# Routed experts on one core: full-width row gathers and scatters without branches, and the down matmul split into high and low parts

## The reference

```python
scores = sigmoid(hf @ w_router); sel = scores + b_router
eidx = top 8 of sel within the best 4 of 8 groups
gw = scores[eidx] / sum * ROUTE_SCALE
for each expert e, with xb = hf[its tokens]:      # xb: n_e x 1024
    u  = silu(xb @ w_gate[e]) * (xb @ w_up[e])    # n_e x 256
    yb = (u @ w_down[e]) * g[:, None]             # n_e x 1024
    y[its tokens] += yb
y += (silu(hf @ ws_gate) * (hf @ ws_up)) @ ws_down
```

## Time and profile before

| | |
|---|---|
| median of 3 runs | 1129.77 us (1128.4 to 1130.07) |
| the profiled execution's own time | 1132.51 us |
| its span in the trace | 1130.7 us |
| mean granted TensorE clock | 0.972 |
| PE busy | 1037.0 us (92%) |
| DVE busy | 836.9 us (74%) |
| ACT busy | 521.8 us (46%) |
| POOL busy | 234.5 us (21%) |
| DMA, all queues | 297.60 MB, 263 GB/s in the mean |
| scatters on the chain that ended last | 28% of the span |

### The profile page before, as it was taken

One profiled execution on the slowest core, in us unless ns is written; L12 is line 12 of the kernel. 1 busy time (PEld: TensorE's weight loads), 2 busy tenths in 40 slices (PEclk: granted clock), 3 DMA queues, 4 the chain that ended last, 5 costly groups with the idle time before them and its releaser, 6 DMA issues.

```text
span 1130.7 us, 16022 instructions
## 1 busy us (share of the span) xinstructions
PE 1037.0 (92%) x4777; PEld 733.0 (65%) x4778; DVE 836.9 (74%) x1480; ACT 521.8 (46%) x610; POOL 234.5 (21%) x145
## 2 busy tenths in 40 slices
PE   1899997978998989999998999999999999899995
PEld 1898887657446447766775666667766666566662
DVE  4887899886665457787876787778787776676865
ACT  3425463364111145555554554555555454545542
POOL 0000000100000034353321323423222222342210
PEclk9899998989996999999999999999999999999998
DMA  9775300600948078999999999999999999999944
GB/s 358 244 277 178 101 1 1 229 14 13 388 186 327 27 249 269 356 344 343 338 366 348 323 333 344 345 337 329 324 338 333 346 308 339 304 328 334 340 113 152
DMA packets 82999, 297.60 MB, mean 263 GB/s; under 512 B 10799, under 2 KB 23131, under 8 KB 73437
## 3 DMA queue, kind: packets, MB, share of 16 engines
q1 hardware_dynamic: 69188, 259.12, 63.6%
q0 software_dynamic: 12208, 34.62, 13.4%
q10 hardware_dynamic: 1514, 2.97, 0.7%
HBM read 274.71 MB, written 24.12 MB: 264 GB/s over the span
## 4 chain that ended last, share of the span: by engine, by line
DMA 37%; PE 13%; issue 7%; POOLq 3%; DVE 3%; SPq 2%; ACT 1%; POOL 0%; DVEq 0%; ACTq 0%
DMA y_rows<-yb,row_numbers 28%; PE ps L2034 6%; DMA side<-in_w_exp_up 5%; PE ps L2089 4%; DMA main<-in_w_exp_up 2%; POOLq L1757 2%; DMA xg<-h_rows,row_numbers 1%; SPq L1573 1%; PE ps L2024 1%; PE ps L2134 1%; POOLq L1751 1%; ACT w_gate_up_hi L1802 1%; DVE main L2008 0%; DVE w_gate_up_lo L1901 0%; DVE pick L1881 0%
## 5 line engine op out<-in xcount | busy, mean ns | idle before, releaser
L1901 DVE TENSOR_TENSOR w_gate_up_lo<-side,w_gate_up_hi 128x2048 fp32r<-128x2048 f32 x64 | 146.8, 2294 | 78.9 <-ACT w_gate_up_hi L1802 78.8
L1901 DVE TENSOR_TENSOR w_gate_up_lo<-main,w_gate_up_hi 128x2048 fp32r<-128x2048 f32 x64 | 146.7, 2292 | 71.9 <-ACT w_gate_up_hi L1802 71.8
L1594 POOL DMA_INDIRECT y_rows<-yb,row_numbers x62 | 116.2, 1874 | 375.3 <-issue 311.4
L1802 ACT ACTIVATE w_gate_up_hi<-side 128x2048 fp32r<-128x2048 f32 x64 | 122.1, 1910 | 95.5 <-DMA side<-in_w_exp_up 54.1
L1802 ACT ACTIVATE w_gate_up_hi<-main 128x2048 fp32r<-128x2048 f32 x64 | 122.2, 1910 | 91.5 <-PE ps L2034 45.8
L2034 PE MATMUL ps<-w_gate_up_hi,xT_hi 128*128 128x512 f32 x512 | 144.7, 404 | 11.8 <-DVE xT_lo L1905 8.7
L2034 PE MATMUL ps<-w_gate_up_hi,xT_lo 128*128 128x512 f32 x512 | 137.6, 390 | 0.0
L2034 PE MATMUL ps<-w_gate_up_lo,xT_hi 128*128 128x512 f32 x512 | 137.3, 390 | 0.0
L2034 PEld LDWEIGHTS ps<-w_gate_up_hi,xT_hi 128*128 128x128 f32 x512 | 91.4, 189 | 32.1 <-issue 14.2
L2034 PEld LDWEIGHTS ps<-w_gate_up_hi,xT_lo 128*128 128x128 f32 x512 | 96.2, 188 | 21.1
L2034 PEld LDWEIGHTS ps<-w_gate_up_lo,xT_hi 128*128 128x128 f32 x512 | 96.1, 188 | 21.0
(11 more groups left out here) (309 smaller groups left out, 1554.9 us busy)
## 6 DMA issues: line engine op xcount, KB each, us to landing
side<-in_w_exp_gate SPq DMA_DIRECT2D x60, 512.0 KB, 9.6
side<-in_w_exp_up SPq DMA_DIRECT2D x60, 512.0 KB, 23.9
main<-in_w_exp_gate SPq DMA_DIRECT2D x60, 512.0 KB, 9.9
main<-in_w_exp_up SPq DMA_DIRECT2D x60, 512.0 KB, 24.6
side<-in_w_ada SPq DMA_DIRECT2D x20, 1024.0 KB, 7.7
main<-in_w_exp_down SPq DMA_DIRECT2D x16, 1024.0 KB, 23.1
maskb<-in_w_exp_down SPq DMA_DIRECT2D x16, 1024.0 KB, 20.4
side<-in_w_exp_down SPq DMA_DIRECT2D x16, 1024.0 KB, 23.6
```

What stands on the lines that cost most here:

```text
L1594: return pool.indirect_dma_start(out=G.y_sums, out_offset=bass.IndirectOffsetOnAxis(ap=sidx[0:rows, n:n + 1], axis=0), in_=yb[0:rows, slot ...
L1802: nc.scalar.activation(whi[:, half], wgu[n % RING][:, :, HALF * half:HALF * (half + 1), :] .rearrange("p m c f -> p c m f"), ACT.Copy).the ...
L1901: nc.vector.tensor_tensor(wlo[:, half], src, whi[:, half].bitcast(F32), ALU.subtract).then_inc(s_wlo, 1)
```

## The change

1. Gathers and scatters always have 128 rows. The scatter gets a bound as well, so that surplus rows are left out. `by_size`, the table of counts and its copy go, and with them the load of the count and all branches in GpSimd's loop.
2. The down matmul is made of three fp32r passes, as gate and up are. ScalarE makes the high parts of the transposed u (`uhi`) and of the down weights (`wdh`, one buffer), VectorE the low parts (`ulo`, and `wdl`, which overwrites the landed weights in their slot). TensorE waits for the low part of the weights; the high part of the next expert's weights waits until the down matmul is done. Twelve matmuls take the place of four.
3. ScalarE writes all 1024 columns of `yb`; VectorE's half and its semaphore go.
4. `pick` is built by one instruction of 512 columns in place of four of 128.

```diff
-MEAN = SEQ * 8 // E_N
-
-SIZES = [*range(MEAN - 16, CAP, 8), CAP]
...
-            nc.vector.tensor_copy(G.count_tab[:, :], n_e[0:1, :])
...
-        uT = sb("uT", [P, 2, FC, CAP])
+        uhi = sb("uT_hi", [P, FC, CAP], FR)
+        ulo = sb("uT_lo", [P, FC, CAP], FR)
+        wdh, wdl = G.w_down_hi, G.w_down_lo
...
-        def gather_rows(pool, slot, n, rows=CAP):
-
-            return pool.indirect_dma_start(out=xg[slot][0:rows, :], out_offset=None, in_=G.h2_rows,
-                                           in_offset=bass.IndirectOffsetOnAxis(ap=sidx[0:rows, n:n + 1], axis=0),
+        def gather_rows(pool, slot, n):
+
+            return pool.indirect_dma_start(out=xg[slot], out_offset=None, in_=G.h2_rows,
+                                           in_offset=bass.IndirectOffsetOnAxis(ap=sidx[:, n:n + 1], axis=0),
                                            bounds_check=SEQ - 1, oob_is_err=False)
...
-        def add_rows(pool, slot, n, rows=CAP):
-
-            return pool.indirect_dma_start(out=G.y_sums, out_offset=bass.IndirectOffsetOnAxis(ap=sidx[0:rows, n:n + 1], axis=0),
-                                           in_=yb[0:rows, slot, :], in_offset=None, compute_op=ALU.add)
+        def add_rows(pool, slot, n):
+
+            return pool.indirect_dma_start(out=G.y_sums, out_offset=bass.IndirectOffsetOnAxis(ap=sidx[:, n:n + 1], axis=0),
+                                           in_=yb[:, slot, :], in_offset=None, compute_op=ALU.add,
+                                           bounds_check=SEQ - 1, oob_is_err=False)
...
-                def by_size(count, sizes, move):
-
-                    if len(sizes) == 1:
-                        move(sizes[0])
-                        return
-                    half = len(sizes) // 2
-                    with pool.If(count > sizes[half - 1]):
-                        by_size(count, sizes[half:], move)
-                    with pool.Else():
-                        by_size(count, sizes[:half], move)
-
-                def count_of(e):
-                    return pool.value_load(G.count_tab[0:1, bass.ds(e, 1)], min_val=0, max_val=SEQ)
-
                 def step(t, n, ahead):
                     e = UNROLL * t + n
                     if ahead(AHEAD):
                         pool.wait_ge(s_idx, e + AHEAD + 1)
                         pool.wait_ge(s_xp, e + 1)
                         pool.sem_inc(s_passed, 1)
-                        count = count_of(e + AHEAD)
-                        by_size(count, SIZES, lambda rows: gather_rows(pool, n % RING, (n + AHEAD) % UNROLL, rows).then_inc(s_g[n % RING], 16))
+                        gather_rows(pool, n % RING, (n + AHEAD) % UNROLL).then_inc(s_g[n % RING], 16)
                     if ahead(2):
                         pool.wait_ge(s_ya, e + 2)
-                        pool.wait_ge(s_yd, e + 2)
                         pool.wait_ge(s_sc, SC0 + 16 * e)
                         pool.sem_inc(s_passed, 1)
-                        count = count_of(e)
-                        by_size(count, SIZES, lambda rows: add_rows(pool, n % 2, n, rows).then_inc(s_sc, 16))
+                        add_rows(pool, n % 2, n).then_inc(s_sc, 16)
...
+                def uT_high(e, slot):
+                    act.wait_ge(s_ut, e + 1)
+                    nc.scalar.activation(uhi[:, :, :], ps[:, 2 + slot, 0:FC * P].rearrange("p (f t) -> p f t", f=FC), ACT.Copy).then_inc(s_uTh, 1)
+
+                def high_down(t, n):
+                    act.wait_ge(s_wd[n % RING], 16 * (UNROLL // RING * t + n // RING) + 16)
+                    if not (isinstance(t, int) and t == 0 and n == 0):
+                        act.wait_ge(s_dn, UNROLL * t + n)
+                    nc.scalar.activation(wdh[:, :, :], wd[n % RING], ACT.Copy).then_inc(s_wdh, 1)
...
-                    nc.scalar.activation(yb[:, n % 2, 0:512], ps[0:CAP, 4, :], ACT.Copy,
+                    nc.scalar.activation(yb[:, n % 2, :].rearrange("p (a b) -> p a b", a=2), ps[0:CAP, 4:6, :], ACT.Copy,
                                          scale=found[:, n, 1:2]).then_inc(s_ya, 1)
+                    if ahead(1):
+                        uT_high(e + 1, (n + 1) % 2)
+                        high_down(t, n + 1)
...
-                    for i in range(NT):
-                        ins = nc.vector.tensor_scalar(pick[:, slot, i, :], k[:, K_IOTA:K_IOTA + CAP],
-                                                      posm[:, bass.ds(NT * e + i, 1)], None, ALU.is_equal)
-                    ins.then_inc(s_pick, 1)
+                    full = [P, NT, CAP]
+                    place_of = posm[:, bass.ds(NT * e, NT)].rearrange("p (i o) -> p i o", o=1).broadcast_to(full)
+                    iota = k[:, K_IOTA:K_IOTA + CAP].rearrange("p (o t) -> p o t", o=1).broadcast_to(full)
+                    nc.vector.tensor_tensor(pick[:, slot], iota, place_of, ALU.is_equal).then_inc(s_pick, 1)
...
-                    dve.wait_ge(s_ut, e + 1)
-                    nc.vector.tensor_copy(uT[:, slot], ps[:, 2 + slot, 0:FC * P].rearrange("p (f t) -> p f t", f=FC)[:, :, 0:CAP]
-                                          ).then_inc(s_uTd, 1)
+                    dve.wait_ge(s_uTh, e + 1)
+                    nc.vector.tensor_tensor(ulo[:, :, :], ps[:, 2 + slot, 0:FC * P].rearrange("p (f t) -> p f t", f=FC),
+                                            uhi[:, :, :].bitcast(F32), ALU.subtract).then_inc(s_uTd, 1)
+
+                def low_down(e, slot):
+                    dve.wait_ge(s_wdh, e + 1)
+                    nc.vector.tensor_tensor(wdl[slot][:, :, :], wd[slot], wdh[:, :, :].bitcast(F32), ALU.subtract).then_inc(s_wdl, 1)
...
-                    dve.wait_ge(s_dn, e + 1)
-                    dve.wait_ge(s_sc, 16 * e + (SC0 - 16))
-                    nc.vector.tensor_scalar(yb[:, n % 2, 512:D], ps[0:CAP, 5, :], found[:, n, 1:2], None, ALU.mult).then_inc(s_yd, 1)
                     if ahead(1):
                         copy_uT(UNROLL * t + (n + 1), (n + 1) % 2)
+                        low_down(UNROLL * t + (n + 1), (n + 1) % RING)
...
-                    pe.wait_ge(s_wd[n % RING], 16 * ((UNROLL // RING) * t + (n // RING + 1)))
+                    pe.wait_ge(s_wdl, e + 1)
                     pe.wait_ge(s_uTd, e + 2)
                     pe.wait_ge(s_ya, e + 1)
-                    pe.wait_ge(s_yd, e + 1)
                     for half in range(2):
                         for f in range(FC):
-                            ins = nc.tensor.matmul(ps[0:CAP, 4 + half, :], uT[:, n % 2, f, :],
-                                                   wd[n % RING][:, f, 512 * half:512 * (half + 1)], start=f == 0, stop=f == FC - 1)
+                            for j, (up, wp) in enumerate(((uhi, wdh), (ulo, wdh), (uhi, wdl[n % RING]))):
+                                ins = nc.tensor.matmul(ps[0:CAP, 4 + half, :], up[:, f, :], wp[:, f, 512 * half:512 * (half + 1)],
+                                                       start=f == 0 and j == 0, stop=f == FC - 1 and j == 2)
...
+        G.w_down_hi = nc.alloc_sbuf_tensor_at("w_down_hi", [P, FC, D], FR, offset=main_at + 4 * (G.QKC + 2048))
+        G.w_down_lo = [nc.alloc_sbuf_tensor_at(f"w_down_lo{n}", [P, FC, D], FR, offset=at)
+                       for n, at in enumerate((side_at + 4 * 8192, main_at + 4 * G.QKC, maskb_at, rows_at + 4 * D))]
```

More of the change, by code:

```diff
@@ L1621, in stage_experts @@
             s_dn = isem("down_done")
-            s_ya = isem("y_low_ready")
-            s_yd = isem("y_high_ready")
+            s_ya = isem("y_ready")
+            s_uTh = isem("uT_high_part")
+            s_wdh = isem("w_down_high_part")
+            s_wdl = isem("w_down_low_part")
             s_sc = isem("scattered")
@@ L1838, in _ @@
                 high_half(0, 1, 1)
+                uT_high(0, 0)
+                act.wait_ge(s_sdn, NT)
+                high_down(0, 0)
                 def step(t, n, ahead):
@@ L1935, in _ @@
                 copy_uT(0, 0)
+                low_down(0, 0)
                 def step(t, n, ahead):
```

8 lines of the change are left out of this document (4 added, 4 removed).

## The result

The changed kernel takes 1172.68 us in the median, against 1129.92 us for the kernel before in the same runs: a ratio of 1.037, with 95% between 1.035 and 1.039. It is 43 us slower. The forecast was 1216 us: the sign and the mechanism came, the size is half.

The account below looks back on a forecast made before the run. It took full DMA engines (10.8 us per expert) as the bound, with a scatter chain nearly as long. From 1132.5 us: +87 for 58 experts, end -2, start +1 gave 1218.5; 2.7 less for the median, 1216. Range 1150 to 1280.

Parts of the forecast that it names:

- rival A: Gathers and scatters: 128 rows put the valid rows on half of the DMA engines; the forecast, 1216 us, chance 0.66.
- The branches: GpSimd's loop: count load, conversion and branches between landing and next scatter go, 0.96 us less per turn.
- I take 12.3 us, between the two: Loop over experts: new period chosen between chain and load prices, ends 11.2 and 13.2; +87 us over 58 experts.
- the price by the load: Busiest DMA engines: small queue doubled to 4.74 us beside the weights' 8.62, less overlap, 13.1 us per expert; or 12.7.
- the price by the chain: Serial scatters: 12.64 us of the 88-row experts less 0.96 us of branches, a period of 11.7 us.
- rival D: Loop: only the chain's price holds, at its low end, a period of 11.2 us; 1152 us, chance 0.08.
- The end: Last three experts, after the loads: the three-pass down matmul saves 2 us.
- so it is just hidden: Before the down matmul: 5.6 us of yb, high and low parts covered by TensorE's 5.48 and 1.4 us of other work.
- TensorE was to wait for weights: Loop: sign that the forecast was right, TensorE waiting more for weights; no size given.
- would be the next bound: VectorE, 9.7 us per expert: hidden under 12.3 us, but without that cover 1.1 us below today's period.
- B: 128 rows spread evenly over the engines: landings stay 8.6 us, chain 9.5; about 1122 us, chance 0.14.
- C: A scatter's out-of-bounds rows are real reads and writes: 13.3 us per expert, +145, 1275 us; chance 0.12.

Follow-up runs that it names:

- e3: Changed kernel with token rows permuted so that the valid rows spread over all sixteen groups of eight rows; 1080.1 us, ratio 0.956.
- e6: Changed kernel with another permutation, tokens going to twelve of the sixteen groups of eight rows first; 1123.8 us, ratio 0.990.
- e4: Changed kernel with the count's load and the branches put back ahead of each scatter, all still 128 rows; 1216.4 us, ratio 1.076.
- e7: Changed kernel with two buffers of sums, for even and odd experts, so a scatter waits only for the one before the last; 1176.4 us, ratio 1.043.
- u1: Changed kernel with sized gathers and scatters, count and branches put back, keeping the three-pass down matmul; 1136.3 us, ratio 1.006.
- u2: Kernel before with only the 128-row transfers, bound and no branches; down matmul stays fp32; 1166.5 us, ratio 1.031.
- e5: Kernel before with 128-row transfers, bound, no branches and the permuted rows of e3; down matmul stays fp32; 1100.7 us, ratio 0.974.
- e9: Kernel before with six transfer widths in steps of 16 in place of eleven in steps of 8; 1122.2 us, ratio 0.993.
- e8: Kernel before with two buffers of sums, one for even and one for odd experts; 1138.3 us, ratio 1.009.
- e10: e5 with the count's load and branches back ahead of each 128-row scatter; four times: 1134.6, 1133.4, 1137.9 and 1109.0 us.
- e12: The kernel of e10 run again; twelve times between 1114.4 and 1144.8 us, median 1134.4 us.

## Why the prediction was right, and where not

**The mechanism of rival A holds.** That 128 rows are cut by their number, with the tokens on one half of the engines, was read from one gather and from the jump between 80 and 88 rows. e3 shows it: the same transfers with the tokens in other rows are 92.6 us faster, and e6 shows it by degrees. The landing was to be 10 to 11 us and is 10.6; large and small experts were to be alike and are; the bytes were to stay and did. That no experiment looked at a single engine's queue remains: the runs show that the cost goes by groups of eight rows, laid out as in the lists of e3 and e6. That such a group is a DMA engine, and not something else that serves these partitions, isn't shown by them.

**The branches**: 0.96 us per turn was forecast, and 1.9 - 0.87 = 1.0 came. e4, which puts them back, has the gap at 1.93 us again.

**What failed is the price of the period**, the step "I take 12.3 us, between the two". It came out at 11.39, and of 87 us in the loop 35 came. The step gave the price by the load half the weight, and that price was far too high; the price by the chain, taken from the landings, would have been right. The two prices under it failed differently.

- By the load, 13.1 or 12.7 us were forecast, and e7, which has only the load left, shows 11.34. The term that made it wrong is the 2.37 us of the small queue, doubled to 4.74 and added to the weights' 8.62. Such a share of busy time is no fixed cost: the same weights take 0.744 x 11.34 = 8.44 us of every engine in e7 and 0.800 x 9.82 = 7.86 in e3, and the small queue 2.05 and 2.21. Even with e7's own shares the sum would be 8.44 + 2 x 2.05 = 12.5 us, 1.2 above what e7 took. The likely reason is the one that the prediction named as a doubt, that the share counts twice what packets of two queues wait for each other on one engine; no view shows that directly. Taking the weights at their undisturbed 7.98 us, e7 leaves (11.34 - 7.98)/8 = 0.42 us for each token on the busiest engine. This estimate gives 7.98 + 5.8 x 0.42 = 10.4 us for e6, where 10.56 was measured.
- By the chain, 12.64 us of the 88-row experts less the branches made 11.7; the other reading in the prediction, a landing of 10.2 us plus 0.95, made 11.2, rival D's period. The landings of all eight, 10.55 us in the mean, with the 0.87 us that was left behind them make 11.42, where 11.39 was measured. The distances of single experts can hold more than a landing and a gap: expert 57 has 14.62 us with a landing of 11.3. The landings themselves were the better base, and the two that the prediction used were a little short.

Rival D came nearest (a period of 11.2 us, 1152 us), for a reason that only half holds: chain and load both come to 11.3 to 11.4 us. e7 takes the chain away and the period stays; e4 lengthens the chain and the period follows. Nothing in the prediction makes the two meet, so that D came near is in part luck.

**The end** was forecast at -2 us and came at +4.2. The faster matmuls were counted (3.04 for 3.45 us) and the casts ahead of them weren't: "so it is just hidden" was worked out for a turn of the loop, with 5.48 us of gate and up beside it, and the last two experts have no such turn. They stand in the open twice, 4.1 us each, the second one behind the last scatter. u1, with +4.8 us in the same place, and u2, with -0.6, show that it belongs to the split alone.

**TensorE was to wait for weights.** It doesn't: ScalarE, which gets the weights first, waits 11.8 and 11.5 us in 640 for gate and up, and what holds it is the landing of the scatter of e-2, through `yb` (134.8 us). TensorE gets this through ScalarE's queue; its own waits are for parts of x, u and the down weights, the longest 38.1 us for `xT_lo`. The prediction had only GpSimd waiting for scatters. The DMA share was to be 0.85 and is 0.94, which goes with the period: 0.94 x 11.39 = 10.7 us per expert would be 0.87 of 12.3.

**The costs beside it** were near: `pick` 0.68 us (0.6 forecast), `yb` 1.12 (1.02), the high part of u 0.38 (0.4), the low part of the down weights 2.29 (2.29), VectorE 422.23/500 x 11.39 = 9.6 us per expert (9.7), ScalarE 8.1 (8.6). That VectorE "would be the next bound" without the cover was nearly right: in e3 it is busy 97.8% of 9.82 us, TensorE 99.4%.

**Rivals B and C** fell by their premises: B's landing of 8.6 us is that of e5, which has the rows spread, and C's extra work didn't come, since the small queue's share fell from 21.9% to 18.2% with 13382 packets under 512 B.

**Open** is why the sized transfers of the kernel before cost the engines what they do. At a share of 1.02 it moved 334 GB/s where e5 moved 359 with the same fp32 matmul. e9 and the landings by width show that the widths are a part. Taking away the chain (e8) shortens the period by 0.1 us only, spreading the rows with the branches kept (e10, e12) brings nothing that can be told, and spread rows without the branches (e5) 29 us. So I read it as two limits of nearly the same height. How rows of 56, 72 or 88 are laid on the engines wasn't tried, and neither was the kernel before with its branches gone and nothing else.

e3 is the version to use: 1080.1 us, 4.4% below the kernel before.

## What to carry to other kernels

A padded transfer isn't paid for by its bytes but by its fullest engine: when only the first n of 128 rows are valid, permute the rows so that any n of them are spread, before judging a change to full width. If two limits lie within a few per cent, undoing one shows nothing; take both away, or make one longer, to see which is there. And look at the last turns of a pipeline by themselves: what a neighbour hides in the loop has no neighbour at the end.

## What the runs showed of the hardware

- The DMA share isn't a measure of work left over: 1.02 goes with 334 GB/s (before), 359 (e5) and 373 (e3) in the same 500 us.
- Rows beyond the bound add little to what the engines are busy with: half as many packets more per expert, but 0.182 x 11.39 = 2.07 us of the small queue per expert, against 2.37 before.
- The busiest group of eight rows sets the landing of a scatter beside a stream of weights: 8.7 us with four tokens in it, 10.8 with eight (e6).
- The down matmul of the last expert took 4.55 us and that of the last but one 3.04, the same twelve instructions. From 1139 to 1144 us the granted clock was 0.69, between its levels of 1.2 and 2.4 GHz, after TensorE had waited 5.37 us for the low part; from 1131 to 1134 us it was 1.00. The rows of the kernel after:

```profile
1131.00:1134.00 3.00, 2.41 (x12) 1.84 (x10) 0.21 (x2) 0.78 (x1) 1.11 (x1) 1.00 0.04 8
1134.00:1139.00 5.00, 0.22 (x1) 0.22 (x2) 2.99 (x4) 2.40 (x3) 0.44 (x1) 0.97 0.43 62
1139.00:1144.00 5.00, 5.00 (x14) 3.67 (x15) 0.51 (x3) 0.63 (x1) 0.00 (x0) 0.69 0.73 279
```

So the exposed casts cost their own 4.1 us and 1.5 us of a slower matmul behind them.
